# Multiplying the sub-keys into the query weights once, in a one-core mixer and product-key expert kernel

## The chip, the cores and the metric

The kernel runs on one core of a Trainium2 chip. The metric is the time of one execution on the device, in microseconds (us), as the median of the runs; lower is better.

## What is computed

One layer over 1,152 tokens (128 of a prompt, 1,024 of a sample), model width 1,024, all in float32. The part that matters here is the routing of the last block, which picks experts by product keys:

```python
def peer(h, w_pq, sub_keys, u_tab, v_tab):          # 8 heads, 2 halves of 128, 128 sub-keys, top 16
    q = (hf @ w_pq).reshape(T, PEER_HEADS, 2, PEER_HALF)
    s = jnp.einsum('thsd,hskd->thsk', q, sub_keys)   # scores: T x 8 x 2 x 128
    s_top, i_top = lax.top_k(s, PEER_TOPK)
    cand_s = s_top[:, :, 0, :, None] + s_top[:, :, 1, None, :]
    f_s, f_pos = lax.top_k(cand_s.reshape(T, PEER_HEADS, 256), PEER_TOPK)
    ...                                              # 128 experts for each token, softmax weights,
                                                     # gelu(u_tab[ids] @ x) weighted sum of v_tab[ids]
```

Before it stand the two mixers (a spatial-gating MLP and an attention with low-rank keys and values), the output product w_o, and a layer norm.

## The kernel before

The program has three parts, one behind the other, with a barrier between them. The work is written out by hand: each engine has its own order of steps, and semaphores join them.

**The mixers** (`mixer_inputs`). TensorE (PE) first makes the first third of the modulation from `w_mod` (four chunks of 2 MB, L545), then the keys and values of the cached context (`keys` L459, `values` L465), then for each of nine tiles of 128 tokens `project` (L481: z = h @ w_in, into banks 0 to 3) and `finish`. SyncE (SP) loads everything in the order of L236 to L252. From the point where the modulation is there, GpSimd (POOL) fills two large scratch tensors in DRAM with zeros (L279, 32 transfers of 768 KB, and L285, 16 of 512 KB), four of them in flight at a time. After the first tile ScalarE (ACT) stores two small outputs (L447, L448) and waits for them.

**The middle** (`middle`) is a loop over slots: slot n = 4i + h is head h of the attention of tile i. Beside the attention (`dots`, `turned`, `values`), each slot carries a piece of the later work of earlier tiles, in a fixed order on every engine: at h = 0 the product with w_o (`mix`, L846: 8 products of 512 columns for each half), at h = 2 the turning of the normed tile (`turn` L854, evicted by ACT's `modulate` L1038), and the routing in four groups g of four sub-key lists each:

- `query(i, g)`, L872: 32 products of 128 columns that give the queries turned, evicted by ACT into `qs` (L1052);
- `score(i, g)`, L882: 4 products of `qs` with the sub-keys `sub`, evicted by ACT into `s` (L1059);
- `lists(i, g)` on VectorE (DVE), L1265 and on: the top 16 of each list; and `decode(i)` at h = 0 of a later tile.

Groups 0 and 1 have their queries at h = 3, group 2 at h = 1, group 3 at h = 2. The score of groups 0 and 3 stands at h = 3, that of 1 at h = 0 of the next tile, that of 2 at h = 2. Banks 6 and 7 are used in turn by all of these steps, so each waits for the eviction of the step before the last. The weights of a step (2 MB: `w_mod2`, `w_o` or `w_pq`) are loaded by SP into one of two halves of `work`, when the step before the last has used it.

In `decode`, ACT's `spread` (L1070) copies list numbers for it; `norm` (L1105) scales an attention output that PE turns first thing in the next slot (L907). POOL places finished tiles' weights into the zeroed scratch with indirect DMAs (L161). At the end of this part PE's `scatter` (L943) and DVE's `one_hot` (L1371 to L1378) make two more tiles' blocks.

**The experts** (`experts`) stream the tables u and v through PE (L1624, L1638) and are not touched.

Of the kernel before, what the change touches and what calls it, by code (L numbers as in the profile page):

```python
# [15 lines left out]
F32 = mybir.dt.float32  # L16
# [7 lines left out]
P = 128  # L24
# [88 lines left out]
def build(nc, a):  # L113
# [11 lines left out]
    with es:  # L125
        x1_dram = nc.dram_tensor("x1_scratch", [T, D], F32, kind="Internal").ap()
        g_dram = [nc.dram_tensor("g_blocks", [CB, P, NKEY, TB], F32, kind="Internal").ap(),
                  nc.dram_tensor("g_cells", [GRID, 1], F32, kind="Internal").ap()]
# [39 lines left out]
def mixer_inputs(nc, a, sb, sem, PS, ident, modc, sp1, silu, slots, carry, work, big, krT, kT, vv, g_dram):  # L168

    with ExitStack() as c:  # L170
# [40 lines left out]
        hs = [hT[:, :, :], hT1]  # L211
        zero = free[:, D:D + ZW]
# [5 lines left out]
        ml = [sem(f"a_m{k}") for k in range(NM)]  # L218
        kl, zl = sem("a_kv"), [sem(f"a_in{n}") for n in range(len(Z))]
# [13 lines left out]
        with nc.Block() as block:  # L233
            @block.sync
            def _(sp):
# [195 lines left out]
            def _(act):  # L431
# [11 lines left out]
                act.activation(vv[:, 1, :], PS[6][:, :], ACT.Copy).then_inc(v_ev, 1)  # L443
                act_gelu(act, 0)
# [84 lines left out]
            def _(pe):  # L529
# [24 lines left out]
                values(pe, cckT)  # L554
                project(pe, 0, 0, first=True)
# [13 lines left out]
def middle(nc, a, sb, sem, PS, ident, modc, sp1, silu, slots, carry, work, first_in, big, krT, kT, vv, x1_dram, gate_dram, g_dram, placed):  # L569
# [7 lines left out]
    def number(*key):  # L577
        W[key] = len(W)
        if key[0] in ("mod", "mix", "query"):
            WEIGHTS.append(key)  # L580

    for n in range(NSLOT):
# [13 lines left out]
        if h == 0:  # L596
            if 0 <= i - 2 < NT:
                number("score", i - 2, 1)
            if 0 <= i - 1 < NT:
                number("mix", i - 1, 0)  # L600
                number("mix", i - 1, 1)
# [30 lines left out]
    with ExitStack() as c:  # L632
        wr = work[:, :].rearrange("p (b c) -> p b c", b=2)
        sub = sb(c, "sub", [P, HS, NKEY])
# [21 lines left out]
        qs = sb(c, "qs", [P, 2, 4, P])  # L656
# [63 lines left out]
        with nc.Block() as block:  # L720

            @block.sync
            def _(sp):
                def load(*key):
# [3 lines left out]
                    name = {"mod": "w_mod2", "mix": "w_o", "query": "w_pq"}[key[0]]  # L728
                    sp.dma_start(wr[:, at % 2, :], a[name][key[-1], :, :]).then_inc(wr_in[at % 2], 16)
# [7 lines left out]
                for n in range(NSLOT):  # L737
# [7 lines left out]
                    if n == 0:  # L745
                        for dst, src in ((ln_g, "ln1_g"), (ln_b, "ln1_b")):
                            sp.dma_start(dst[:, :], a[src]).then_inc(const_in, 16)
                        sp.dma_start(sub[:, :, :], a["sub"]).then_inc(const_in, 16)
# [5 lines left out]
                    if h == 1 and 0 <= i - 2 < NT:  # L754
                        load("query", i - 2, 2)
                    if h == 2 and 0 <= i - 2 < NT:
                        load("query", i - 2, 3)
                    if h == 3 and 0 <= i - 1 < NT:
                        load("query", i - 1, 0)
                        load("query", i - 1, 1)  # L760
# [10 lines left out]
                sp.wait_ge(w_mm, W["query", LAST, 3] + 1)  # L771
# [29 lines left out]
            def _(pe):  # L801
# [62 lines left out]
                def query(i, g):  # L864
# [3 lines left out]
                    w, ps = weights("query", i, g), bank("query", i, g)  # L868
                    for l in range(4):
                        for k in range(DK):  # L870
                            at = (l * DK + k) * P
                            mm = pe.matmul(ps[:, l * P:(l + 1) * P], w[:, at:at + P], slots[:, i, k * P:(k + 1) * P],  # L872
                                           start=(k == 0), stop=(k == DK - 1))
                    mm.then_inc(w_mm, 1)

                def score(i, g):
                    ps = bank("score", i, g)
                    pe.wait_ge(*emptied("query", i, g))
                    if i == 0 and g == 0:
                        pe.wait_ge(const_in, 48)  # L880
                    for l in range(4):
                        mm = pe.matmul(ps[:, l * NKEY:(l + 1) * NKEY], qs[:, g % 2, l, :], sub[:, 4 * g + l, :],  # L882
                                       start=True, stop=True)
# [64 lines left out]
                for n in range(NSLOT):  # L948
# [21 lines left out]
                    if h == 0:  # L970
                        if 0 <= i - 2 < NT:
                            score(i - 2, 1)
                        if 0 <= i - 1 < NT:
                            mix(i - 1, 0)
                            mix(i - 1, 1)
                    if h == 1 and 0 <= i - 2 < NT:
                        query(i - 2, 2)
                    if h == 2:
                        if 0 <= i - 2 < NT:
                            score(i - 2, 2)  # L980
# [3 lines left out]
                        if 0 <= i - 2 < NT:  # L984
                            query(i - 2, 3)
                    if h == 3:
                        if 0 <= i - 2 < NT:
                            score(i - 2, 3)
# [3 lines left out]
                        if 0 <= i - 1 < NT:  # L992
                            query(i - 1, 0)
                            query(i - 1, 1)
                            score(i - 1, 0)
                    if n == NH + 2:
# [9 lines left out]
            def _(act):  # L1006
# [38 lines left out]

                def query(i, g):
                    ps, f = bank("query", i, g)
                    n = 4 * i + g
                    if n >= 2:
                        p = ("score", (n - 2) // 4, (n - 2) % 4)  # L1050
# [1006 lines left out]
```

## Time and profile before

| what | value |
| --- | --- |
| median of 3 runs | 3407.02 us (3401.91 to 3409.48) |
| the profiled execution | 3406.51 us, its span 3404.4 us |
| PE busy over the span | 3273.6 us (96%) |
| DVE, POOL, ACT busy | 2590.0, 1564.4, 1238.5 us |
| the mixers | 0 to about 363 us |
| the middle | about 363 to 1233 us |
| the experts | about 1233 to 3404 us |
| L872 (queries), PE | 2304 instructions, busy 263.5 us |
| memory read, written | 888.70 MB, 61.24 MB |

The span is the time from the first to the last instruction; some 2 us of the execution lie around it. A float32 product is two instructions in the trace (32 products are x64). The end of a product is modelled, so the pace of PE is read from the start of one group to the start of the next.

### The profile page before, as it was taken

To read this page: it belongs to the slowest core of one execution; us is meant where nothing else is said; L and a number is where in the kernel's file an instruction comes from. 1 tells how busy PE (TensorE), PEld (TensorE's weight loads), DVE (VectorE), ACT (ScalarE), POOL (GpSimd) and SP (SyncE) were. 2 spreads that over 40 slices of the span, in tenths; PEclk is the share of its full clock that TensorE was granted. 3 is DMA by queue.
4 is the path that set the end of the run, shared out by engine and by line. 5 is a ranking of instruction groups with operands and counts; after the bars stand their busy time and mean duration, and the time that the engine had idled before them with its cause. 6 is when DMAs were issued, how large, how long until landed. Compare 5 with 4: busy or idle time off the path is not lost.

```text
span 3404.4 us, 46351 instructions
## 1 busy us (share of the span) xinstructions
PE 3273.6 (96%) x17054; PEld 2753.7 (81%) x17054; DVE 2590.0 (76%) x5319; ACT 1238.5 (36%) x2289; POOL 1564.4 (46%) x969
## 2 busy tenths in 40 slices
PE   8999899999998779999999999999999999999997
PEld 3566358777876769999898999998999999999996
DVE  0232126888887879999999898889899998888866
ACT  1232233333432653333333333333433333333333
POOL 1100000578876428888788888433233332222201
PEclk9999999999999989999999999999999999999998
DMA  9600535666666579999999999998898999999943
GB/s 395 250 21 8 211 149 192 180 178 194 165 183 184 176 278 352 343 347 358 336 348 344 356 361 357 381 356 345 353 374 342 368 371 350 358 350 350 349 160 121
DMA packets 290762, 952.91 MB, mean 280 GB/s; under 512 B 92905, under 2 KB 146281, under 8 KB 231793
## 3 DMA queue, kind: packets, MB, share of 16 engines
q1 hardware_dynamic: 154322, 513.36, 40.6%
q0 software_dynamic: 135936, 436.53, 37.2%
q8 instruction: 132, 2.16, 0.2%
q14 instruction: 84, 0.69, 0.1%
q10 hardware_dynamic: 288, 0.16, 0.0%
HBM read 888.70 MB, written 61.24 MB: 279 GB/s over the span
## 4 chain that ended last, share of the span: by engine, by line
PE 57%; DVE 4%; DMA 2%; issue 0%; ACT 0%; SPq 0%; DVEq 0%; ACTq 0%
PE bank L1624 29%; PE bank L1638 28%; DMA work<-in_u 2%; DVE ring L1751 1%; DVE uL L1937 1%; DVE acc L1768 0%; DVE vL L1932 0%; DVE ga L1964 0%; ACT uR L1711 0%; DVE slots L1873 0%; DMA work<-x_scratch 0%; DVE cL L1929 0%; DVE st L1897 0%; DVE slots L1894 0%; DVE slots L1912 0%
## 5 line engine op out<-in xcount | busy, mean ns | idle before, releaser
L1585 POOL DMA_INDIRECT ring<-in_uv,slots x384 | 583.3, 1519 | 799.4 <-DVE carry L1768 686.6
L161 POOL DMA_INDIRECT g_cells<-slots x384 | 703.0, 1831 | 379.2 <-DVE slots L1350 260.5
L1624 PE MATMUL bank<-hR,uR 128*128 128x384 f32 x2048 | 690.1, 337 | 19.2 <-DVE uL L1937 19.2
L1624 PE MATMUL bank<-hR,uL 128*128 128x384 f32 x2048 | 690.0, 337 | 0.0
L1624 PE MATMUL bank<-hL,uR 128*128 128x384 f32 x2048 | 688.2, 336 | 0.0
L1697 ACT ACTIVATE cR<-ga 128x384 fp32r<-128x384 f32 x256 | 134.6, 526 | 946.2 <-PE bank L1638 691.0
L1638 PE MATMUL bank<-vR,cR 128*128 128x512 f32 x1536 | 477.5, 392 | 0.7 <-DVE slots L1873 0.7
L1638 PE MATMUL bank<-vR,cL 128*128 128x512 f32 x1536 | 476.0, 391 | 0.0
L1638 PE MATMUL bank<-vL,cR 128*128 128x512 f32 x1536 | 475.7, 391 | 0.0
L1751 DVE CUSTOM_DVE_ANT_0 ring<-ring,slots 128x1024 f32<-128x1024 f32 x384 | 467.7, 1255 | 0.0
L1624 PEld LDWEIGHTS bank<-hR,uR 128*128 128x128 f32 x2048 | 386.6, 189 | 31.1 <-DVE uL L1937 21.3
L1624 PEld LDWEIGHTS bank<-hL,uR 128*128 128x128 f32 x2048 | 386.4, 189 | 9.6
L1624 PEld LDWEIGHTS bank<-hR,uL 128*128 128x128 f32 x2048 | 385.9, 188 | 0.0
L1638 PEld LDWEIGHTS bank<-vL,cR 128*128 128x128 f32 x1536 | 288.3, 188 | 64.4
L1932 DVE TENSOR_TENSOR vL<-work,vR 128x1024 fp32r<-128x1024 f32 x256 | 313.1, 1223 | 34.1 <-ACT vR L1703 33.5
L1638 PEld LDWEIGHTS bank<-vR,cL 128*128 128x128 f32 x1536 | 288.2, 188 | 62.8
L1768 DVE SCALAR_TENSOR_TENSOR carry<-ring,cs,carry 128x1024 f32<-128x1024 f32 x254 | 326.4, 1285 | 9.1
L1937 DVE TENSOR_TENSOR uL<-work,uR 128x1024 fp32r<-128x1024 f32 x256 | 312.0, 1219 | 24.8 <-ACT uR L1711 24.7
L1638 PEld LDWEIGHTS bank<-vR,cR 128*128 128x128 f32 x1536 | 284.7, 188 | 44.2 <-issue 1.0
L1711 ACT ACTIVATE uR<-work 128x1024 fp32r<-128x1024 f32 x256 | 267.6, 1046 | 22.8 <-DMA work<-in_u 20.4
L872 PE MATMUL bank<-slots,work 128*128 128x128 f32 x2304 | 263.5, 276 | 7.3 <-ACT slots L1038 6.2
L872 PEld LDWEIGHTS bank<-slots,work 128*128 128x128 f32 x2304 | 260.3, 193 | 10.2 <-issue 8.0
(290 smaller groups left out, 4107.0 us busy)
## 6 DMA issues: line engine op xcount, KB each, us to landing
work<-in_u SPq DMA_DIRECT2D x256, 512.0 KB, 6.5
work<-in_v SPq DMA_DIRECT2D x256, 512.0 KB, 7.1
work<-in_w_pq SPq DMA_DIRECT2D x36, 2048.0 KB
work<-in_w_o SPq DMA_DIRECT2D x18, 2048.0 KB
g_cells<-work POOLq DMA_DIRECT2D x32, 768.0 KB, 7.3
work<-g_blocks SPq DMA_DIRECT2D x32, 768.0 KB, 13.5
work<-g_cells SPq DMA_DIRECT2D x32, 768.0 KB, 9.1
work<-in_w_mod SPq DMA_DIRECT2D x8, 2048.0 KB
```

The source lines that it names most:

```text
L161: pool.indirect_dma_start(out=cells_of(g_dram, i), out_offset=bass.IndirectOffsetOnAxis(ap=slots[:, i, D + k:D + k + 1].bitcast(U32), axis=0),
L872: mm = pe.matmul(ps[:, l * P:(l + 1) * P], w[:, at:at + P], slots[:, i, k * P:(k + 1) * P], start=(k == 0), stop=(k == DK - 1))
L1585: pool.indirect_dma_start(out=ring[:, k % R, :], out_offset=None, in_=a["uv"], in_offset=bass.IndirectOffsetOnAxis(ap=ids[:, k // P, k % P ...
L1624: mm = pe.matmul(A[t][:, 0:CW], w[:, t, k, :], h[:, k, :], start=(k == 0 and w is uR and h is hR), stop=(k == DK - 1 and w is uL))
L1638: mm = pe.matmul(ACC[2 * tt + half][:, :], w[:, t, tt * P:(tt + 1) * P], v[:, t, half * 512:(half + 1) * 512], start=(m == 0 and w is cR a ...
L1697: act.activation(cR[:, x % 2, :], ga[:, x % 2, :], ACT.Copy).then_inc(c_r, 1)
L1711: act.activation(uR[:, x % 2, :, :], uw[:, x % 2, :, :], ACT.Copy).then_inc(u_r, 1)
L1751: dve.tensor_tensor_reduce(out=ring[:, k % R, 0:D], in0=ring[:, k % R, 0:D], in1=whole(STILES[k // P]), scale=1.0, scalar=0.0, op0=ALU.mul ...
L1768: dve.scalar_tensor_tensor(accS[t], ring[:, k % R, D:2 * D], one, accS[t], ALU.mult, ALU.add).then_inc(v_done, 1)
L1932: dve.tensor_tensor(vL[:, x % 2, :], vw[:, VBUF[x], :], vR[:, x % 2, :].bitcast(F32), ALU.subtract).then_inc(v_l, 1)
L1937: dve.tensor_tensor(uL[:, x % 2, :, :], uw[:, x % 2, :, :], uR[:, x % 2, :, :].bitcast(F32), ALU.subtract).then_inc(u_l, 1)
```

## The change

The sub-keys are multiplied into the query weights once. Since s = (h @ w_pq) @ sub, the product w_pq @ sub of each list is formed in the mixers, behind `values` of the cached context and ahead of the first `project`, and written to a new scratch tensor in DRAM of 8 MB (`keys_scratch`). It is made in eight pieces of 1 MB: PE forms four banks of 512 columns of each piece (4 products of 128 columns a bank), ACT evicts them, stores the piece, and issues the load of the piece after the next. In the middle `query` and `qs` go; `score(i, g)` is now 8 products of 512 columns over the 1,024 model columns with the stored product as the moving operand, 2 MB of it loaded where `w_pq` was. Scores stand where the queries of the same group stood; lists and decoding stay in their slots. The load of `sub` moves from the middle to the mixers, ahead of `w_in`.

```diff
+                  nc.dram_tensor("keys_scratch", [4, P, DK * 512], F32, kind="Internal").ap()]
...
+        NPIECE = 8
+        piece = [flat[:, 8192:10240], big[:, 6144:8192]]
+        folded = [flat[:, b * 2048:(b + 1) * 2048] for b in range(2)]
+        sub = big[:, 8192:10240].rearrange("p (l k) -> p l k", l=HS)
...
(SP, mixers, behind the loads of w_kn, cckT, w_v)
+                sp.wait_ge(m_used, 2)
+                for p in range(2):
+                    sp.dma_start(piece[p], a["w_pqT"][p, :, :].rearrange("p (l d) -> p l d", l=4)).then_inc(ml[p], 16)
+                sp.wait_ge(m_used, 3)
+                sp.dma_start(sub[:, :, :], a["sub"]).then_inc(ml[2], 16)
                 for n, (at, w) in enumerate(Z):
                     sp.dma_start(w_in[:, :, at:at + w], a["w_in"][:, :, at:at + w]).then_inc(zl[n], 16)
...
(ACT, mixers)
+                for b in range(4 * NPIECE):
+                    p, k = divmod(b, 4)
+                    act.wait_ge(m_used, NM + b + 1)
+                    if k == 0 and p >= 2:
+                        act.wait_ge(fold_out[p % 2], fold_first[p % 2] + p // 2 * 16)
+                    act.activation(folded[p % 2][:, k * 512:(k + 1) * 512], PS[b % 4][:, :],
+                                   ACT.Copy).then_inc(m_row, 1)
+                    if k == 3:
+                        act.wait_ge(m_row, NM + b + 1)
+                        g, half = divmod(p, 2)
+                        act.dma_start(g_dram[2][g, :, half * 2048:(half + 1) * 2048], folded[p % 2]).then_inc(
+                            fold_out[p % 2], 16)
+                        if p + 2 < NPIECE:
+                            act.dma_start(piece[p % 2], a["w_pqT"][p + 2, :, :].rearrange(
+                                "p (l d) -> p l d", l=4)).then_inc(ml[p % 2], 16)
+                for k in range(2):
+                    act.wait_ge(fold_out[k], fold_first[k] + NPIECE // 2 * 16)
                 act_gelu(act, 0)
...
(PE, mixers)
                 values(pe, cckT)
+                pe.wait_ge(ml[2], 32)
+                for p in range(NPIECE):
+                    pe.wait_ge(ml[p % 2], (p // 2 + 2) * 16)
+                    for k in range(4):
+                        b = 4 * p + k
+                        pe.wait_ge(m_row, max(NM, NM + b - 3))
+                        for l in range(4):
+                            mm = pe.matmul(PS[b % 4][:, l * NKEY:(l + 1) * NKEY], piece[p % 2][:, l, k * P:(k + 1) * P],
+                                           sub[:, 4 * (p // 2) + l, :], start=True, stop=True)
+                        mm.then_inc(m_used, 1)
+                pe.wait_ge(m_row, NM + 4 * NPIECE)
                 project(pe, 0, 0, first=True)
...
(the order of the middle's steps; PE, ACT and SP follow it)
-            if 0 <= i - 2 < NT:
-                number("score", i - 2, 1)
...
         if h == 1 and 0 <= i - 2 < NT:
-            number("query", i - 2, 2)
+            number("score", i - 2, 2)
         if h == 2:
-            if 0 <= i - 2 < NT:
-                number("score", i - 2, 2)
...
             if 0 <= i - 2 < NT:
-                number("query", i - 2, 3)
+                number("score", i - 2, 3)
         if h == 3:
-            if 0 <= i - 2 < NT:
-                number("score", i - 2, 3)
...
             if 0 <= i - 1 < NT:
-                number("query", i - 1, 0)
-                number("query", i - 1, 1)
                 number("score", i - 1, 0)
+                number("score", i - 1, 1)
...
(PE, middle)
-                def query(i, g):
+                def score(i, g):
                     if g == 0:
                         pe.wait_ge(*emptied("turn", i, 0))
                         pe.wait_ge(*emptied("turn", i, 1))
...
+                    w, ps = weights("score", i, g), bank("score", i, g)
+                    for k in range(DK):
+                        mm = pe.matmul(ps[:, :], slots[:, i, k * P:(k + 1) * P], w[:, k * 512:(k + 1) * 512],
+                                       start=(k == 0), stop=(k == DK - 1))
                     mm.then_inc(w_mm, 1)
...
(ACT, middle: query and its evictions into qs go; the score evictions move with the scores)
-                    act.activation(qs[:, g % 2, :, :], ps[:, :].rearrange("p (l t) -> p l t", l=4),
-                                   ACT.Copy).then_inc(f, 1)
...
-        "w_pq": n["w_pq"][0].reshape(DK, P, 4, 4, P).transpose(2, 1, 3, 0, 4).reshape(4, P, 4 * DK * P),
+        "w_pqT": n["w_pq"][0].reshape(2, 512, 4, 4, P).transpose(2, 0, 4, 3, 1).reshape(8, P, 4 * 512),
```

## Rows read from the trace of the kernel before

**Rows 1.** Busy time by window in the middle; the first line names the columns.

```profile
core 0: us, PE busy (x) PEld busy (x) DVE busy (x) ACT busy (x) POOL busy (x), PEclk, DMA share, GB/s
765.00:850.00 85.00, 83.92 (x526) 65.85 (x526) 69.87 (x311) 29.97 (x73) 71.29 (x46) 1.00 0.70 195
1020.00:1105.00 85.00, 68.51 (x482) 58.13 (x483) 67.64 (x320) 23.95 (x51) 58.69 (x38) 0.92 0.63 179
```

**Rows 2.** Waits of PE from 510 to 1020 us: total us, times, longest.

```profile
PE bank L872 <- ACT slots L1038: 5.0, 6, 0.8
PE bank L854 <- ACT carry L1059: 1.8, 7, 0.3
```

**Rows 3.** Timeline of PE over one tile: start us, us, instruction.

```profile
753.21 1.06 PE L882 MATMUL bank<-sub,qs 128*128 128x128 f32 x8
754.10 3.60 PE L846 MATMUL bank<-work,slots 128*128 128x512 f32 x8
...
760.97 3.60 PE L846 MATMUL bank<-work,slots 128*128 128x512 f32 x8
...
774.81 7.31 PE L872 MATMUL bank<-slots,work 128*128 128x128 f32 x64
781.96 0.27 PE L907 MATMUL bank<-ident,on 128*128 128x128 f32 x1
...
789.83 0.60 PE L854 MATMUL bank<-ident,xr 128*128 128x128 f32 x4
...
792.17 7.38 PE L872 MATMUL bank<-slots,work 128*128 128x128 f32 x64 [0.83 <-ACT slots L1038]
```

**Rows 4.** Timeline of ACT in the same tile.

```profile
780.30 0.37 ACT L1105 ACTIVATE on<-bank,ri 128x128 f32<-128x128 f32 x1
...
787.78 1.06 ACT L1070 ACTIVATE key<-itb 128x1024 bf16<-128x1024 bf16 x1 [0.16 <-DVE itb L1276]
```

**Rows 5.** Timeline of DVE in the same tile.

```profile
808.52 0.87 DVE L1265 MAX8 top<-carry 128x8 f32<-128x128 f32 x4 [3.36 <-ACT carry L1059]
```

**Rows 6.** Timeline of PE at the end of the middle.

```profile
1065.45 7.41 PE L872 MATMUL bank<-slots,work 128*128 128x128 f32 x64 [1.06 <-DMA work<-in_w_pq]
...
1136.14 3.81 PE L943 MATMUL bank<-big,krT 128*128 128x128 f32 x32 [2.23 <-ACT krT L1132]
```

**Rows 7.** Timeline of PE in the mixers.

```profile
43.43 3.65 PE L459 MATMUL bank<-cckT,work 128*128 128x128 f32 x16 [0.58 <-DVE sp L377]
...
48.64 23.36 PE L481 MATMUL bank<-w_in,carry 128*128 128x512 f32 x64
...
100.90 1.95 PE L459 MATMUL bank<-ckT,work 128*128 128x128 f32 x16
...
122.64 7.83 PE L481 MATMUL bank<-w_in,carry 128*128 128x384 f32 x14 [3.69 <-DVE work L333]
```

**Rows 8.** Windows of 4 us in the mixers (the last two columns: DMA share, GB/s).

```profile
60.00:64.00 4.00, 4.00 (x12) 1.91 (x11) 0.80 (x4) 0.60 (x1) 1.07 (x2) 1.00 1.01 422
136.00:140.00 4.00, 3.93 (x34) 3.74 (x33) 2.81 (x10) 0.00 (x0) 0.00 (x0) 1.00 0.34 134
```

**Rows 9.** DMA, 0 to 170 us: POOL's queue (packets, MB, share); issues (KB, us to landing).

```profile
q0 software_dynamic: 6912, 33.56, 48.8%
...
g_cells<-work POOLq DMA_DIRECT2D x32, 768.0 KB, 7.3
...
out_new_krope<-kr ACTq DMA_DIRECT2D x1, 32.0 KB, 11.1
```

**Rows 10.** DMA queues, 55 to 56 us: packets, MB, share of the engines' time.

```profile
q0 software_dynamic: 45, 0.26, 61.6%
q1 hardware_dynamic: 45, 0.17, 40.5%
```

**Rows 11.** DMA queues, 108 to 109 us.

```profile
q0 software_dynamic: 27, 0.14, 49.2%
q1 hardware_dynamic: 74, 0.20, 48.7%
```

More of the change, by code:

```diff
@@ L578, in number @@
         W[key] = len(W)
-        if key[0] in ("mod", "mix", "query"):
+        if key[0] in ("mod", "mix", "score"):
             WEIGHTS.append(key)
@@ L727, in load @@
                         sp.wait_ge(w_mm, W[WEIGHTS[at - 2]] + 1)
-                    name = {"mod": "w_mod2", "mix": "w_o", "query": "w_pq"}[key[0]]
-                    sp.dma_start(wr[:, at % 2, :], a[name][key[-1], :, :]).then_inc(wr_in[at % 2], 16)
+                    src = {"mod": a["w_mod2"], "mix": a["w_o"], "score": g_dram[2]}[key[0]]
+                    sp.dma_start(wr[:, at % 2, :], src[key[-1], :, :]).then_inc(wr_in[at % 2], 16)
                 def load_x(i):
@@ L754, in _ @@
                     if h == 1 and 0 <= i - 2 < NT:
-                        load("query", i - 2, 2)
+                        load("score", i - 2, 2)
                     if h == 2 and 0 <= i - 2 < NT:
-                        load("query", i - 2, 3)
+                        load("score", i - 2, 3)
                     if h == 3 and 0 <= i - 1 < NT:
-                        load("query", i - 1, 0)
-                        load("query", i - 1, 1)
+                        load("score", i - 1, 0)
+                        load("score", i - 1, 1)
                         sp.wait_ge(x1_ready, i)
@@ L770, in _ @@
                             sp.dma_start(gate_dram[m, :, :], gl[:, m, :]).then_inc(gate_out, 16)
-                sp.wait_ge(w_mm, W["query", LAST, 3] + 1)
+                sp.wait_ge(w_mm, W["score", LAST, 3] + 1)
                 for k in range(2):
@@ L969, in _ @@
                                 second(2 * n)
[L970 to L975, printed above, removed]
+                    if h == 0 and 0 <= i - 1 < NT:
+                        mix(i - 1, 0)
+                        mix(i - 1, 1)
                     if h == 1 and 0 <= i - 2 < NT:
-                        query(i - 2, 2)
+                        score(i - 2, 2)
                     if h == 2:
-                        if 0 <= i - 2 < NT:
-                            score(i - 2, 2)
                         if 0 <= i - 1 < NT:
@@ L984, in _ @@
                         if 0 <= i - 2 < NT:
-                            query(i - 2, 3)
+                            score(i - 2, 3)
                     if h == 3:
-                        if 0 <= i - 2 < NT:
-                            score(i - 2, 3)
                         if i - 2 in STILES:
@@ L992, in _ @@
                         if 0 <= i - 1 < NT:
-                            query(i - 1, 0)
-                            query(i - 1, 1)
                             score(i - 1, 0)
+                            score(i - 1, 1)
                     if n == NH + 2:
@@ L1148, in _ @@
                         root(i - 1)
-                    if h == 2:
-                        if 0 <= i - 2 < NT:
-                            score(i - 2, 2)
-                        if 0 <= i - 1 < NT:
-                            modulate(i - 1, 0)
-                            modulate(i - 1, 1)
+                    if h == 2 and 0 <= i - 1 < NT:
+                        modulate(i - 1, 0)
+                        modulate(i - 1, 1)
                     if n + 1 < NH:
@@ L1166, in _ @@
                             use(2 * n)
-                    if h == 0 and 0 <= i - 2 < NT:
-                        score(i - 2, 1)
                     if h == 1 and 0 <= i - 2 < NT:
-                        query(i - 2, 2)
+                        score(i - 2, 2)
                     if h == 2 and 0 <= i - 2 < NT:
-                        query(i - 2, 3)
+                        score(i - 2, 3)
                     if h == 3:
-                        if 0 <= i - 2 < NT:
-                            score(i - 2, 3)
                         if i - 2 in STILES:
@@ L1179, in _ @@
                         if 0 <= i - 1 < NT:
-                            query(i - 1, 0)
-                        if 0 <= i - 1 < NT:
-                            query(i - 1, 1)
                             score(i - 1, 0)
+                            score(i - 1, 1)
                     if n == NH + 2:
```

42 lines of the change are left out of this document (10 added, 32 removed).

## The prediction

> **What bounds the kernel now.** I first cut the span into windows. In the middle the busy time of PE is 83.92 of 85 us at full clock, that of DVE 69.87, of ACT 29.97; near its end, from 1020 us, PE has only 68.51 [rows 1]. A busy PE can hide waits, so I read its waits next: from 510 to 1020 us they come to 6.8 us in all, 1.3% [rows 2]. So the loop over slots is set by PE's pace until the last tile, and what PE no longer does there is gained, unless another engine's chain comes up from behind. In the mixers I looked at PE's timeline and at the DMAs: PE goes on without a gap at 48.64 us into the first `project` [rows 7], while the transfers, POOL's zeros above all, fill the DMA engines (422 GB/s, share 1.01) until about 137 us [rows 8]. The zeros cost nothing today, for PE needs no transfer then. The change puts eight loads and eight stores of 1 MB on PE's path just there. So it gives in one part and takes in another, and the question is which is larger.
>
> **What the middle gains.** A group of queries is 64 instructions, from 774.81 to 781.96: 7.15 us [rows 3]. The new score of a group has the form of a half of `mix`, 8 float32 products of 512 columns with a token tile as the stationary operand: 754.10 to 760.97, 6.87 us [rows 3]. That is 0.28 us less, 36 times (9 tiles, 4 groups): 10.1 us. The old score goes: 753.21 to 754.10, 0.89 us, 36 times: 32.0 us. Together 42.1 us. The columns that stream are the same in the old query and the new score, 4,096 a group; this is why an edit that halves the steps gives 15% of them and not half.
>
> ACT loses 36 evictions; PE waited for none of them inside the loop [rows 2], so that is worth nothing but for the two waits named below. DVE no longer waits for the score of group 3 (3.36 us in this tile [rows 5]); that gives DVE slack.
>
> Two things take back from the 42.1:
> - At h = 2 PE turns the tile at 789.83 and starts the next group at 792.17 [rows 3], when ACT has evicted the first half. ACT comes to it from `spread`, 787.78 to 788.84 [rows 4], which hangs on DVE's chain. PE will be there 1.17 us earlier than now against that chain (0.89 + 0.28 since h = 0) and loses the score as well, so ACT is late: first half out at about 790.4, where PE alone would be some 0.3 us earlier. 7 tiles: 2 us.
> - In the tail a stretch is DVE's (layer norm of the last tile, then its lists), so the 1.17 us of one query and score are lost; the last score stands behind the first `scatter` at 1136.14, from which DVE's pace counts, 0.9 lost; and loads get tight: the one for 1065.45 already comes 1.06 us late [rows 6], and group 2 of the last tile is now needed some 6.9 us after its buffer is free instead of 8.9, so 1 us. Waits for `qs` that go give 1.4 back. Net 1.7 us.
>
> So the middle gains 42.1 − 2 − 1.7 = 38 us. Bounds: 42 if nothing is lost, 22 in a rival below.
>
> **What the mixers pay.** Nothing of the fold runs beside other PE work. Piece 0 is there in time: SP issues it when the second chunk of `w_mod` is used. Its products begin where `project` does now, at 48.6. A piece is 32 instructions of 128 columns, half of a query group: 3.6 us at full clock. PE alone would take 8 × 3.6 = 29 us. But pieces 2 to 7 come through ACT's queue, each behind a store: up to the landing of piece 7 the order is six pairs of store and load, 12 transfers of 1.05 MB. The first can start when piece 0 is made (52.2) and evicted, about 53; a load begins to move some 2 us after its issue, so I count from 55. With the engines to themselves each would take 1.05 MB at 422 GB/s = 2.5 us; but POOL always has four zero transfers in flight. How two queues share is seen when `xT` is loaded beside the zeros: 40.5% against 61.6% of the engines' time in one microsecond [rows 10], 48.7% against 49.2% in another [rows 11]. Half of the bandwidth gives 5.0 us a transfer. In the first of these, both queues got 45 packets, so the larger packet gets more: rows of 8 KB beside zeros of 6 KB would have 57%, 4.4 us. I take 4.7, in the middle between them: 12 × 4.7 = 56 us, piece 7 at 111.4.
>
> By the Trainium skill (DMA: Bandwidth & Descriptors, section Queues, rings and completion order) an engine goes round the queues by packets. The trace's 45 to 45 agrees and its 27 to 74 does not; by that rule alone the sum would be 12 × 0.3 = 4 us lower.
>
> PE now stands still some microseconds for each piece, and after such a pause it runs at the lower of its two clocks: 16 instructions of L459 took 3.65 us at 43.43, where the granted clock had fallen, and 1.95 at 100.90 [rows 7]. So piece 7 takes about 7 us: the fold ends at 118.4 and adds 118.4 − 48.6 = 70 us. Bounds: 43 with the engines to itself (12 × 2.5, and 7), 89 in the rival of the long queue.
>
> The first `project` may start at the low clock: 0 to 4 us, I take 2. The last two stores need not be waited for by PE: ACT waits for them, and its first gelu is needed only by the second `project`, 23 us later [rows 7]. SP issues `w_in` (7 MB) only when the third chunk of `w_mod` is used; at 0.42 MB/us it needs 17 us and has 70; the fold hides it, and would not if it took under some 10 us. The zeros end later: 14.7 MB of ACT's queue (eight stores, six loads) at 0.42 MB/us is 35 us, and what is left of `w_in` some 7, so near 179 instead of 137, still long before POOL is needed in the middle. That has a good side. Today ACT's small store of the first tile falls among the zeros, lands after 11.1 us [rows 9], and PE waits 3.69 us for what is behind it and then runs slowly, 14 products in 7.83 us [rows 7]. With the change this store comes at about 175 to 180, when the zeros are over or nearly so: gain 0 to 7, I take 4.
>
> **The sum.** −38 + 70 + 2 − 4 = +30 us. The experts are untouched. The profiled execution took 3406.5 us (span 3404.4 and 2.1 around it), half a microsecond under the median of 3407.0; from the median it gives 3437 us, 0.9% slower. Its own range is 3425 to 3448 (4.4 to 5.0 us a transfer, and the ends of the small terms). A difference of 0.2%, 7 us, is what a measurement of this kernel can tell from none.
>
> **The rivals.**
> - *The fold's transfers are served first, not slower.* If ACT's queue gets nearly all the bandwidth, the fold adds 43 us: −38 + 43 + 2 − 4 = +3, 3410 us. It decides from a fold of 40 us on down. For it: ACT's packets are larger than the zeros', and up to four transfers of 1 MB are queued. Against it: both shares seen stay under one half. Chance 0.14.
> - *The long queue.* Each transfer waits behind what POOL has in flight. For it: 32 KB took 11.1 us to land, and a zero transfer of 768 KB 7.3 [rows 9]. Then a load behind its store lands after some 11 + 5 + 2 = 18 us, a round of two pieces takes 18 + 7 + 1 = 26, and the fold ends at 53 + 18 + 2 × 26 + 14 = 137: it adds 89, 3456 us. Against it: the queues shared in rows 10 and 11. Chance 0.15.
> - *DVE's chain takes over in the middle.* At the end of h = 1 `norm` is done at 780.67 [rows 4] and PE wants it at 781.96 [rows 3], 1.29 us later. With PE 1.17 us earlier the slack is 0.1. Tiles whose decoding is longer, or ACT a step later, would wait 2 us a tile: 16 us of the gain are lost, 3453 us. Chance 0.10.
> - *Wide products are much cheaper.* If PE's pace is set by the instruction and not by its columns, the 16 instructions of a group at 7.15 / 64 = 0.112 us take 1.8 us, and 36 × 5.1 = 182 us more are gained: 3255 us. Against it: the 16 of L846 take 6.87 us, 0.43 each, four times the columns at four times the time [rows 3]. Chance 0.01. The Trainium skill has a milder form of this (TensorE: Matmul & The Clock Gate, section Back-to-back issue gap: about 131 ns at 512 columns beside 81 ns at 128). By its pair a group would take an estimated 2.9 us and the kernel 3294 us; the row of L846 does not agree.
>
> **Chances.** The forecast has 0.60. Of the first rival 0.05 lies under −0.2% and 0.09 within; with the last one: faster 0.06, within 0.2% 0.10, slower 0.84. The range runs from the first rival to the second, 3410 to 3458, and leaves out the far sides of both.
>
> **What would show it.** Right: L872 and `qs` gone, the score at 6.87 us a group, slots at h = 0 shorter by 0.9 and at h = 3 by 2.3; PE's first L481 near 118 us, with PE waiting for piece loads in between and a low granted clock; ACT's queue with 0.5 to 0.6 of the DMA share. Wrong: `project` before 92 or after 135 us; PE waiting for L1105 or L1038 by over 1 us in each tile.

## The result: 1.2% slower, +38 us

| what | value |
| --- | --- |
| kernel before, median of 4 runs | 3404.53 us (3401.91 to 3409.48) |
| changed kernel, median of 4 runs | 3442.84 us (3440.15 to 3454.76) |
| ratio, estimated from all runs | 1.0118, 95% interval 1.009 to 1.0145 |
| changed kernel again, beside the last experiments, median of 4 runs | 3445.95 us, ratio 1.0121 (1.0105 to 1.0136) |

The forecast was 3437 us, +30, with a range of 3410 to 3458. The profiled execution of the changed kernel was its longest, 3454.76 us (span 3452.8), so the account below has a second profiled execution of the same kernel beside it (3446.86 us). One execution of an experiment below, zeros_late, took 14927.77 us; its median there is of the other four. Each stretch ends where PE starts the first instruction of the next part.

| landmark | before | after | after, second | change | change, second |
| --- | --- | --- | --- | --- | --- |
| first `project` starts | 48.6 | 129.9 | 129.4 | +81.3 | +80.8 |
| first product of the middle's attention | 363.5 | 437.9 | 437.4 | −6.9 | −6.9 |
| first `scatter` | 1136.1 | 1180.3 | 1180.3 | −30.3 | −29.7 |
| experts start | 1238.9 | 1281.7 | 1281.7 | −1.4 | −1.4 |
| span | 3404.4 | 3452.8 | 3444.9 | +5.6 | −2.3 |

The last two columns are what each stretch adds. The first four stretches sum to +42.8 in both profiles. Only the experts, which the change doesn't touch, differ (2171.1 and 2163.2 us), so the 7.9 us between the two profiled executions are theirs.

**The fold.** PE's timeline in the mixers, changed kernel (start us, us, instruction; in brackets the wait before it). L592 is the fold, L511 is `project`, L489 and L495 are the keys and values of the cached context [rows 7]:

```profile
44.88 2.50 PE L489 MATMUL bank<-cckT,work 128*128 128x128 f32 x16 [0.58 <-DVE sp L390]
47.17 3.13 PE L495 MATMUL bank<-work,cckT 128*128 128x512 f32 x4
50.14 3.73 PE L592 MATMUL bank<-big,slots 128*128 128x128 f32 x32
53.71 3.74 PE L592 MATMUL bank<-big 128*128 128x128 f32 x32
68.29 6.34 PE L592 MATMUL bank<-big,slots 128*128 128x128 f32 x32 [10.84 <-DMA slots<-in_w_pqT]
77.96 6.62 PE L592 MATMUL bank<-big 128*128 128x128 f32 x32 [3.32 <-DMA big<-in_w_pqT]
90.08 5.72 PE L592 MATMUL bank<-big,slots 128*128 128x128 f32 x32 [5.50 <-DMA slots<-in_w_pqT]
98.81 3.84 PE L592 MATMUL bank<-big 128*128 128x128 f32 x32 [3.01 <-DMA big<-in_w_pqT]
111.90 6.71 PE L592 MATMUL bank<-big,slots 128*128 128x128 f32 x32 [9.25 <-DMA slots<-in_w_pqT]
122.84 6.38 PE L592 MATMUL bank<-big 128*128 128x128 f32 x32 [4.24 <-DMA big<-in_w_pqT]
129.91 23.47 PE L511 MATMUL bank<-w_in,carry 128*128 128x512 f32 x64 [0.69 <-ACT slots L462]
```

Each piece from the third on waits for its load, six waits and 36.2 us in all. Most waits cost twice: five of the six pieces behind them take 5.7 to 6.7 us, where the first two took 3.73. In stretches of these five the granted clock is 0.50 to 0.67 of full speed; only the piece at 98.81, after a wait of 3.01 us, has the full clock and takes 3.84. The fold takes 79.8 us in all; beside the waits and 29.4 us of products at full clock (no_transfers below) some 14 us are left, nearly all of it the price of the low clock. The windows show the mean granted clock beside full DMA engines (mean clock, DMA share and GB/s are the last three columns):

```profile
54.00:80.00 26.00, 11.84 (x72) 11.46 (x72) 0.00 (x0) 5.07 (x9) 3.19 (x6) 0.68 1.02 422
80.00:106.00 26.00, 14.13 (x89) 13.56 (x87) 0.00 (x0) 7.16 (x12) 3.19 (x6) 0.80 1.02 421
106.00:129.00 23.00, 12.86 (x64) 12.68 (x64) 0.00 (x0) 4.18 (x7) 2.65 (x5) 0.63 1.02 422
```

The engines move 422 GB/s as before [rows 8]. What changed is whose bytes they are. The DMA queues of the changed kernel, first from 54 to 110 us, then in two single microseconds, 92 to 93 and 98 to 99 (columns: packets, MB, share of the engines' time; q0 POOL's zeros, q10 ACT's stores and loads of the fold, q1 SP's loads, what is left of `w_in` and then the smaller ones behind it):

```profile
q0 software_dynamic: 1978, 10.79, 46.1%
q10 hardware_dynamic: 1441, 10.54, 44.6%
q1 hardware_dynamic: 1988, 2.26, 11.1%
...
q10 hardware_dynamic: 31, 0.25, 59.9%
q0 software_dynamic: 28, 0.17, 39.6%
q1 hardware_dynamic: 30, 0.01, 4.8%
...
q0 software_dynamic: 72, 0.39, 94.1%
q1 hardware_dynamic: 70, 0.01, 6.9%
q10 hardware_dynamic: 4, 0.00, 0.2%
```

While all three queues have work, each sends about the same number of packets (31, 30, 28), and ACT's queue, with the largest ones, has 0.25 MB in that microsecond. But over the 56 us it sent 1441 packets, the others 1978 and 1988. While it has work it is not served fewer packets, but it is empty or nearly so at times: at 77 to 79, at 88, and at 98 to 100. By 121 us it has sent 12.57 MB, the 12 transfers up to the load of piece 7, and PE starts that piece at 122.84. ACT's timeline shows why there are gaps:

```profile
54.54 0.35 ACTq L467 DMA_DIRECT2D keys_scratch<-slots  x1
54.93 0.76 ACTq L470 DMA_DIRECT2D slots<-in_w_pqT  x1
...
75.30 0.33 ACTq L467 DMA_DIRECT2D keys_scratch<-slots  x1
75.66 0.47 ACTq L470 DMA_DIRECT2D slots<-in_w_pqT  x1
```

L467 is the store and L470 the load; both are issued when a piece is multiplied and evicted. The first store is issued at 54.54, and ACT's queue sends its first packet between 57 and 58. Later the pair behind piece 2 is issued at 75.3, the older load is through at 77, and the queue sends hardly anything until 79.

**The middle.** PE's timeline in one tile, for [rows 3]; L876 is `mix`, L884 `turn`, L900 the new `score`, L925 stood at L907:

```profile
812.79 3.60 PE L876 MATMUL bank<-work,slots 128*128 128x512 f32 x8
...
826.52 0.27 PE L925 MATMUL bank<-ident,on 128*128 128x128 f32 x1
...
833.50 7.03 PE L900 MATMUL bank<-work,slots 128*128 128x512 f32 x16
840.54 0.30 PE L925 MATMUL bank<-ident,on 128*128 128x128 f32 x1
...
847.54 1.04 PE L884 MATMUL bank<-ident,xr 128*128 128x128 f32 x8
850.22 7.11 PE L900 MATMUL bank<-work,slots 128*128 128x512 f32 x16 [1.64 <-ACT slots L1048]
857.16 0.27 PE L925 MATMUL bank<-ident,on 128*128 128x128 f32 x1
...
864.13 13.90 PE L900 MATMUL bank<-work,slots 128*128 128x512 f32 x32
877.87 0.27 PE L925 MATMUL bank<-ident,on 128*128 128x128 f32 x1
```

Two groups go from 864.13 to 877.87, 6.87 us each. From 580 to 1060 us PE's waits are these, for [rows 2] (total us, times, longest):

```profile
PE bank L900 <- ACT slots L1048: 9.3, 6, 1.7
PE bank L925 <- ACT on L1106: 0.8, 1, 0.8
```

The end of the middle, PE's timeline, for [rows 6]; L891 turns a finished tile back, L961 is `scatter`:

```profile
1127.89 1.94 PE L884 MATMUL bank<-ident,xr 128*128 128x128 f32 x8 [8.57 <-DVE xr L1246]
1136.02 10.05 PE L900 MATMUL bank<-work,slots 128*128 128x512 f32 x16 [6.19 <-ACT slots L1048]
...
1149.11 13.97 PE L900 MATMUL bank<-work,slots 128*128 128x512 f32 x32 [1.70 <-ACT slots L1054]
1164.05 14.00 PE L900 MATMUL bank<-work,slots 128*128 128x512 f32 x32 [0.97 <-DMA work<-keys_scratch]
1180.28 1.91 PE L961 MATMUL bank<-big,krT 128*128 128x128 f32 x15 [2.23 <-ACT krT L1133]
```

For the same stretch of the kernel before, PE's longest waits from 1020 to 1140 us (total, times, longest; L1052 evicts the queries, L1059 the scores):

```profile
PE bank L854 <- ACT carry L1059: 6.0, 1, 6.0
PE bank L882 <- ACT qs L1052: 5.2, 3, 4.1
PE bank L854 <- DVE xr L1254: 2.5, 1, 2.5
```

### The profile page after: what moved, and what is told of

It is laid out like the page before. It is cut to its first block, busy times and chain, and to the rows that moved or that the text cites. A ratio compares the mean times of both kernels' runs of the same rounds, so it can differ in the third digit from the quotient of the medians.

```text
span 3452.8 us, 42789 instructions
## 1 busy us (share of the span) xinstructions
PE 3275.1 (95%) x15294; PEld 2611.3 (76%) x15294; DVE 2590.1 (75%) x5319; ACT 1237.8 (36%) x2285; POOL 1569.3 (45%) x969
## 4 chain that ended last, share of the span: by engine, by line
PE 48%; DVE 9%; DMA 4%; issue 1%; ACT 1%; SPq 0%; DVEq 0%; ACTq 0%
PE bank L1616 24%; PE bank L1630 24%; DMA work<-in_u 3%; DVE ring L1743 2%; DVE acc L1760 2%; DVE uL L1929 1%; DVE vL L1924 1%; DVE ga L1956 1%; DVE cL L1921 0%; ACT uR L1703 0%; ACT vR L1695 0%; DVE slots L1865 0%; DMA work<-x_scratch 0%; DVE st L1889 0%; DVE slots L1886 0%
## 5 line engine op out<-in xcount | busy, mean ns | idle before, releaser
L1703 ACT ACTIVATE uR<-work 128x1024 fp32r<-128x1024 f32 x256 | 267.8, 1046 | 37.8 <-DMA work<-in_u 35.8
L900 PE MATMUL bank<-work,slots 128*128 128x512 f32 x576 | 257.1, 603 | 22.2 <-ACT slots L1048 16.8
L1695 ACT ACTIVATE vR<-work 128x1024 fp32r<-128x1024 f32 x256 | 267.6, 1045 | 0.0
```

What stands on the lines that cost most here:

```text
L900: mm = pe.matmul(ps[:, :], slots[:, i, k * P:(k + 1) * P], w[:, k * 512:(k + 1) * 512], start=(k == 0), stop=(k == DK - 1))
L1695: act.activation(vR[:, x % 2, :], vw[:, VBUF[x], :], ACT.Copy).then_inc(v_r, 1)
L1703: act.activation(uR[:, x % 2, :, :], uw[:, x % 2, :, :], ACT.Copy).then_inc(u_r, 1)
```

## The experiments

Theory A, of the forecast: the change is two independent parts, a gain on PE in the middle and a loss in the mixers; the loss is transfers on PE's path that share the DMA engines with the zeros. Its rivals are that the parts touch each other, and that the fold is held by something else: a delay of each round, or its buffers.

Eleven kernels ran, each beside the kernel before on the same chip (its median: 3403.78 us beside the first four, 3404.07 beside deep_zeros_late and the kernels with swap but no stores4, 3403.39 beside the other three). "Fold" is the time from PE's first fold product to its first `project`; "to the middle" and "to `scatter`" are the next two stretches of the table above, 314.9 and 772.6 us in the kernel before. scores_only and no_transfers leave a part of the computation out.

| kernel | median us | ratio (95%) | fold | first `project` | to the middle | to `scatter` |
| --- | --- | --- | --- | --- | --- | --- |
| fold_only | 3474.16 | 1.0203 (1.0186 to 1.0221) | 79.7 | 129.8 | 308.0 | 772.6 |
| scores_only | 3369.77 | 0.9895 (0.9878 to 0.9911) | none | 49.1 | 314.1 | 740.6 |
| zeros_late | 3422.31 | 1.0049 (1.0033 to 1.0065) | 56.1 | 105.6 | 312.4 | 741.6 |
| no_transfers | 3396.01 | 0.998 (0.9971 to 0.999) | 29.4 | 79.1 | 309.7 | 741.1 |
| deep_zeros_late | 3417.25 | 1.004 (1.0026 to 1.0054) | 48.7 | 98.5 | 313.9 | 740.4 |
| stores4_late | 3416.45 | 1.004 (1.0027 to 1.0054) | 45.2 | 95.1 | 314.1 | 738.1 |
| after_swap | 3434.47 | 1.0089 (1.0073 to 1.0106) | 78.8 | 127.5 | 307.9 | 733.3 |
| before_swap | 3402.72 | 0.9993 (0.9983 to 1.0003) | none | 49.2 | 314.3 | 769.0 |
| deep_late_swap | 3411.54 | 1.002 (1.0011 to 1.003) | 48.1 | 97.2 | 313.9 | 737.5 |
| stores4_late_swap | 3409.61 | 1.0018 (1.0009 to 1.0027) | 44.9 | 94.2 | 314.1 | 733.9 |
| after_again | 3445.95 | 1.0121 (1.0105 to 1.0136) | 79.5 | 129.4 | 308.0 | 742.9 |

### Each part alone: fold_only and scores_only

The first is the kernel before with the fold added and its result used by nothing:

```diff
 (kernel before; SP, PE and ACT get the fold's steps as in the change)
+                pe.wait_ge(ml[2], 32)
+                for p in range(NPIECE):
+                    pe.wait_ge(ml[p % 2], (p // 2 + 2) * 16)
...
                 project(pe, 0, 0, first=True)
```

> The kernel before with the multiplying-in added to its mixers and its result not used: queries and scores stay as they were. Theory A (the whole loss is the fold, which waits for transfers that share the DMA engines with the zeros): the first project begins near 130 us as in the changed kernel, against 48.6; the stretch behind it is some 7 us shorter; total near 3404.5 + 81 - 7 = 3479 us. Rival B (part of what the changed kernel lost lies in its middle, in loading the scores' weights from scratch memory): less than that, 3450 to 3465 us.

The second is the change without the fold:

```diff
-                (the fold's steps on SP, PE and ACT)
...
-                    src = {"mod": a["w_mod2"], "mix": a["w_o"], "score": g_dram[2]}[key[0]]
+                    src = {"mod": a["w_mod2"], "mix": a["w_o"], "score": a["w_pq"]}[key[0]]
```

> The changed kernel without the multiplying-in: no pieces, no sub-keys; the scores' products read the query weights themselves (as many bytes in the same form), so their values are not scores. Theory A: from the first group's product to the first scatter 30 us less than before, from project to the middle as before; total near 3404.5 - 31 = 3373 us. Rival B (the middle gains nothing, or as much as was counted, 38): 3404 or 3366 us.

Measured: +70.4 and −34.0 us, together +36.4, beside +38.3 and +42.6 for the change in its two measurements. The parts add to 2 to 6 us less than the change, whose own two measurements differ by 4. fold_only has its first `project` at 129.8 and scores_only its stretch to `scatter` at 740.6, where the changed kernel has 129.9 and 742.4. What the middle gained and what the fold cost can be read apart.

### The zeros behind the fold: zeros_late

```diff
+                pool.wait_ge(m_row, NM + 4 * NPIECE)
                 for b in range(NZ):
                     if b >= 4:
```

> The changed kernel, with POOL's zero transfers held back until the fold's last eviction. Theory A (shared DMA engines): twelve transfers of 1.05 MB at 2.5 to 3.5 us, with w_in beside the first: project begins at 90 to 97 instead of 130 us; the small store of the first tile falls among the zeros again (7 us back); total near 3443 - 36 + 7 = 3414 us. Rival C (the fold is set by its own chain of landing, products, eviction and issue, with two pieces in the air, whatever else the engines carry): project at 115 us or later, total above 3430 us.

Measured: the first `project` at 105.6, between what the two theories asked for (90 to 97, and 115 or later), and 20 us off the time. PE's timeline:

```profile
66.34 6.41 PE L593 MATMUL bank<-big,slots 128*128 128x128 f32 x32 [9.54 <-DMA slots<-in_w_pqT]
72.70 3.84 PE L593 MATMUL bank<-big 128*128 128x128 f32 x32
81.39 5.74 PE L593 MATMUL bank<-big,slots 128*128 128x128 f32 x32 [4.85 <-DMA slots<-in_w_pqT]
```

The pieces now come in pairs some 15 us apart. The zeros are gone from the fold, and it still waits 19.7 us for loads, while the DMA engines have gaps. So the zeros cost 24 of the fold's 80 us (79.8 − 56.1), and a large part of the rest is not shared bandwidth.

### No transfers: no_transfers

```diff
-                    if k == 0 and p >= 2:
-                        act.wait_ge(fold_out[p % 2], fold_first[p % 2] + p // 2 * 16)
...
-                        act.dma_start(g_dram[2][g, :, half * 2048:(half + 1) * 2048], folded[p % 2]).then_inc(
...
-                            act.dma_start(piece[p % 2], a["w_pqT"][p + 2, :, :].rearrange(
```

> The changed kernel, its fold made from pieces 0 and 1 again and again, with no store and no further load; the scores read the query weights instead (values not scores, same bytes). Theory A: PE makes 256 instructions without a pause, 29 us, project at 79 to 82 us, zeros over at 137; total near 3443 - 49 + 5 = 3399 us. Rival D (ACT's evictions hold the fold up even without transfers): project after 90 us.

The scores read the query weights here, so their values are not scores. PE's last piece:

```profile
74.63 3.74 PE L580 MATMUL bank<-big 128*128 128x128 f32 x32
```

Measured: fold 29.4 us, `project` at 79.1, 3396.0 us. PE's part of the fold is 8 pieces of 3.57 us at full clock, as forecast. The other 50 us of the 80 hang on the transfers: the waits for them and the low clock behind the waits. It is also the bound: with transfers that cost nothing the change would gain 8 us.

### More buffers: deep_zeros_late and stores4_late

Four buffers for the pieces in place of two, all four loads issued at the start by SP, and the zeros late; then four buffers for the folded pieces too.

```diff
-        piece = [x.rearrange("p (l d) -> p l d", l=4) for x in piece]
+        piece = [x.rearrange("p (l d) -> p l d", l=4) for x in piece] + [kT[:, :, 2 * P:6 * P], kT[:, :, 6 * P:10 * P]]
...
-                        if p + 2 < NPIECE:
+                        if p + 4 < NPIECE:
...
 (stores4_late)
-        folded = [flat[:, b * 2048:(b + 1) * 2048] for b in range(2)]
+        folded = [flat[:, b * 2048:(b + 1) * 2048] for b in range(4)]
```

> The changed kernel with the zeros held back and four pieces in the air instead of two: pieces 0 to 3 are loaded from the start, each later one when the piece four before it is evicted. Theory E (beside the zeros, the fold was held by having only two pieces in the air: of the 56 us it took with the zeros held back, 29 are PE's products and the rest the wait for landings): project begins at 80 to 88 us instead of 105.6, total near 3422 - 21 = 3401 us. Rival F (it is bandwidth even so: stores, loads and w_in together fill the engines): project at 98 us or later, total 3415 us or more.

> As deep_zeros_late (four piece buffers, zeros behind the fold), and four buffers for the folded pieces in place of two, so that an eviction waits for a store only from the fifth piece on. Nothing is left out. Theory I (the two store buffers were what held deep_zeros_late back: its evictions waited 4 to 7 us five times for a store): the first project starts at 86 to 92 instead of 98.5, and the time is 6 to 12 us under that of deep_zeros_late, 3405 to 3411. Theory J (its stretch was already filled by transfers: the share of the DMA queues was about 1 up to 88): the project starts at 95 or later and the time is within 3 us of deep_zeros_late.

deep_zeros_late has `project` at 98.5, at theory F's number. But its pieces wait in another place. ACT's and PE's waits in it, from 50 to 130 us:

```profile
ACT slots L465 <- DMA keys_scratch<-slots: 24.8, 5, 7.3
...
PE bank L595 <- ACT slots L465: 12.3, 5, 5.6
```

No piece waits for its load any more; PE waits for an eviction, and that for a store out of one of the two `folded` buffers. I took those for the limit (theory I). stores4_late, with four, takes the wait away and has `project` at 95.1, only 3.4 us earlier, with the time within 1 us: theory J. Its DMA windows say what the limit is by then:

```profile
54.00:70.00 16.00, 14.18 (x112) 13.99 (x111) 0.00 (x0) 7.85 (x15) 0.00 (x0) 0.89 1.04 407
70.00:80.00 10.00, 7.25 (x63) 6.87 (x62) 0.00 (x0) 4.51 (x8) 0.00 (x0) 1.00 1.03 409
80.00:88.00 8.00, 2.33 (x20) 2.13 (x19) 0.00 (x0) 1.79 (x3) 0.00 (x0) 0.93 1.04 401
```

The engines are full up to 88 us with no zeros among the transfers: ACT's queue has 67.5% of them and SP's, with `w_in`, 35.8%. Pieces 4 to 7 still wait for loads, 10.2 us in all, and the last runs at the low clock:

```profile
87.72 6.70 PE L596 MATMUL bank<-big 128*128 128x128 f32 x32 [5.67 <-DMA big<-in_w_pqT]
```

So with the zeros gone and four buffers on each side, the bytes of the fold and of `w_in` leave a fold of 45 us, 16 more than PE needs, and 45 is more than the 32 to 35 that the middle gives (the last column against 772.6).

### The order of two steps on ACT: after_swap, before_swap, deep_late_swap, stores4_late_swap

In the middle PE waits for `modulate` (L1048), which stands behind `spread` at h = 2. Here it stands ahead:

```diff
-                    if 0 <= n - 2 * H - 1 < LAST * H:
-                        spread(*divmod(n - 2 * H - 1, H))
...
                     if h == 2 and 0 <= i - 1 < NT:
                         modulate(i - 1, 0)
                         modulate(i - 1, 1)
+                    if h == 2 and 0 <= n - 2 * H - 1 < LAST * H:
+                        spread(*divmod(n - 2 * H - 1, H))
```

> The changed kernel, with ACT's evictions of the turned tile placed ahead of its spread at h = 2. Theory G (PE's wait for the first half of these evictions, 9.3 us over six tiles and 6.2 in the tail, is ACT's order: spread hangs on DVE's chain): both waits fall to below 1 us a tile, the stretch from the first attention to the first scatter is 10 to 15 us shorter, total near 3443 - 12 = 3431 us. Rival H (DVE's chain gives the pace by then, so the wait moves to norm's output or to the next score): the stretch is shorter by less than 4 us.

> The kernel before with the same swap (its score of group 2 and the turned tile's evictions ahead of spread). Theory G: its waits of 5.0 and 1.8 us over the tiles and 6.0 in the tail fall, total 6 to 12 us less, near 3395 us. Rival H: within 3 us of the kernel before.

> All three together on the changed kernel: zeros held back, four pieces, the swap. If the parts add: 3401 - 12 = 3389 us, under the kernel before by 0.4%. If the swap gives nothing: 3401 us, no difference from before.

> The same with the modulation ahead of the spread on ACT in the middle. Nothing is left out. If the two parts add as they did in deep_late_swap: 5 to 6 us under stores4_late. By theory I that is 3399 to 3405, level with the kernel before; by theory J 3408 to 3414.

In the changed kernel it gives 8.4 us against the first measurement and 11.5 against the second; some 2 us of that are a first `project` that starts earlier, which the swap doesn't touch. In the kernel before it gives 1.3, which its interval can't tell from nothing. The stretch to `scatter` is 9.0 us shorter with it in the changed kernel and 3.7 in the kernel before, so most of what it mends was made by the change. Theory G asked for 10 to 15 us and waits under 1 us a tile, theory H for less than 4: neither came. Most of the gain is not in the loop, where I had looked for it: there the six waits for L1048 only fell from 9.3 to 7.5 us. From the first score to the last tile's slot after_swap gains 2.4 us, from there to `scatter` 6.6. Of these, 5.4 are the wait of 6.19 us at 1136.02 above, which is down to 0.83:

```profile
1124.03 9.58 PE L900 MATMUL bank<-work,slots 128*128 128x512 f32 x16 [0.83 <-issue]
```

In deep_late_swap and stores4_late_swap the swap gives 5.7 and 6.8. deep_late_swap came out at 3411.5 us, above both numbers asked of it (3389 and 3401); stores4_late_swap is at theory J's. These two are the best with the whole computation, and are still 0.2% slower than the kernel before, both intervals above 1. No version with the whole computation beat the kernel before; before_swap can't be told from the kernel before.

### The changed kernel once more: after_again

> The changed kernel once more, unaltered, for a second profiled execution of it beside the one of 3452.8. If that one's 12 us over the median lay in the fold or the middle, the account of the change by stretches has to be redone; if they lay in the experts' stretch (2171.1 there), this one has the first project at 128 to 131, the middle stretch at 741 to 743 and the experts' stretch shorter, 2157 to 2165, and the time is 3438 to 3446.

It came out so in each stretch; the account of the result uses it.

## Why the prediction was right, and where its terms were off

The direction held, and so did the two mechanisms, a gain on PE in the middle and a larger loss to the fold's transfers. The size is +38.3 and +42.6 us where +30 was forecast. It owes something to luck: the fold and the middle missed by 11.3 and 6.4 us in one direction, and the stretch behind the fold by 4.9 in the other. By the prediction's steps:

- **Pace of the new score: right.** 6.87 us a group forecast and measured. The products of 512 columns are no cheaper by the column; the last rival is out. Slots at h = 0 are 20.7 us where 21.6 was, at h = 3 20.7 where 23.05 was: 0.9 and 2.35 less, forecast 0.9 and 2.3. DVE's wait for the score of group 3 is gone.
- **The loop: right, 1 us short.** From the first group to the last tile's slot, 28 queries at 0.28 and 27 scores at 0.89 are 31.9 us; measured 28.8, so 3.1 lost where I had said 2. PE's waits for L1048 went from 5.0 to 9.3 us, at the place named and twice as large; waits of 1.8 for L1059 fell away [rows 2]. At some 1.5 us a tile they are over the 1 us that the prediction had named as a sign of being wrong: here its 0.3 us a tile was too small.
- **The tail: too small a loss.** The remaining 10.2 us of the 42.1 should have lost 1.7 and lost 7.3. PE's waits from the last tile's slot to `scatter` rose from 18.8 to 24.1. The step at fault: I let the last tile's 1.17 us of one group be lost and counted 1.4 us back for waits for `qs` that go. But PE has 4.4 us less to do between the last tile's slot and its turning (three queries at 0.28 and four scores at 0.89), and the stretch takes 54.5 us where it took 52.9. The 5.2 us of waits for `qs` are gone, and the wait for the layer norm has grown from 2.5 to 8.57: PE arrives earlier and waits for the same DVE chain. Behind it PE waits 6.19 for `modulate`, where it had waited 6.0 for L1059; on ACT both stand behind `spread`, which waits for DVE. Then the group runs at the low clock, 10.05 us for 16. Sum of the middle: −31.6 where −38 was forecast.
- **DVE's chain takes over: no.** PE waited once for L1106, 0.8 us. The slack of 0.1 held.
- **Transfers of the fold: the term that was off most.** 12 transfers from 55 us at 4.7 us each were to bring piece 7 at 111.4; it came at 122.8, 11.4 later. At 5.65 us each it looks like a wrong share. The queues say otherwise. The first packet left three microseconds later than I had counted, between 57 and 58. The twelfth transfer was through at about 121, and PE started piece 7 1.8 us later, a delay that I had not counted. Between 58 and 121 ACT's queue was empty for some 5 us in three gaps. What is left, 121 − 58 − 5 = 58 us for 12, is 4.8 each, close to the forecast's 4.7. So of the 11.4 us about 5 are the gaps, 3 the late start, 1.8 the end of the last load, and the rest is pace. The step that failed most is "the order is six pairs of store and load", taken as a queue that always has work. With two piece buffers and two store buffers the next pair is issued only when a piece is through PE and ACT, and with PE at the low clock that comes later than the queue can wait. zeros_late shows it from the other side: without the zeros the queue has still more gaps.
- **The long queue: not its mechanism, but near its number.** The first `project` at 129.9 lies nearer to this rival's 137 than to the forecast's 118.4, and a round of two pieces took 21.8 us, between the forecast's 18.8 and the rival's 26. The loads landed after 14.4 and 19.1 us (medians), as the rival had it (18). But ACT's transfers did not wait behind what POOL had in flight: in the microseconds with work in both queues they sent as many packets. The first rival's 92 is far off; its fold of 43 us is near the 45 of stores4_late, which has no zeros beside it.
- **How queues share.** I took the middle between half by time and a share by packet size. The microsecond shown above has 31, 30 and 28 packets. The Trainium skill (DMA: Bandwidth & Descriptors, section Queues, rings and completion order) says that an engine takes its queues in turn, by packets, and this trace agrees where all three have work. At 0.25 MB in that microsecond a transfer of 1.05 MB would take 4.2 us; but from 112 to 113, with 22, 24 and 25 packets and larger ones on SP's queue, ACT's queue has 0.18 MB, which is 5.8 us. The pace of 4.8 is a mean over both. That a third queue would take its turn beside the two was not in my sum, and over 54 to 110 us ACT's queue has 44.6% of the engines, where I had asked for 50 to 60.
- **Piece 7 at the low clock, 7 us: right** (7.07 to `project`). **The first `project` slow, +2: no**, its 64 products took 23.3 us as before.
- **Behind the fold: −6.9, forecast −2.** PE's wait of 3.7 us and the slow products behind it [rows 7] are gone, 3 us more than I took, and the +2 did not come. That it hangs on the zeros fits zeros_late, where they fall on that stretch again and it is 312.4 instead of 308.0, and scores_only, 314.1.
- **`w_in` and the zeros hidden: right for both.** PE waited for neither. But `w_in` was a third queue beside the fold: it was issued from 34.9 us on instead of 6.4, and its last part landed 56.1 us after its issue. In stores4_late SP's queue, with `w_in`, had 35.8% of the engines. What the fold takes without it was not tried. The zeros ended near 178 us, forecast 179.

Summed: the fold +11.3 and the middle +6.4 above the forecast, the stretch behind −4.9: +12.8, so +42.8 for what the change touches. The medians say +38.3 and +42.6.

Open: whether the three gaps would close with deeper buffers while the zeros stay where they are; the two were only tried together. And the gaps' 5 us are counted from single microseconds of one profile. Why the waits of the loop hardly shrank with the swap is open too.

## What to carry to other kernels

A precomputation that saves PE time on every tile must itself find cover: here 34 us saved in the middle were paid with 80 us in a place where PE had been running without a gap and the DMA engines were full. Before costing a chain of load, compute and store by bandwidth, ask how many transfers are issued ahead, since each one that waits for the compute adds its delay, and a wait of PE can bring the low clock for the next piece, here in five of six. And where two waits in a row hang on one slow chain, removing the first gives nothing and only lengthens the second, as with the waits for `qs` and for the layer norm here.

## What the runs showed of the hardware that was not expected

- Three DMA queues on the same engines sent about the same number of packets in a microsecond (31, 30 and 28), whatever their size, so bytes go by packet size: 0.25, 0.01 and 0.17 MB.
- From the issue of ACT's first store of 1 MB (54.54 us) to the first packet of its queue (57 to 58 us) about 3 us passed, with other queues busy; and from the last bytes of the load of piece 7 (about 121) to PE's first product of it (122.84) 1.8 us.
- The untouched stretch of the experts took 2171.1 and 2163.2 us in two profiles of one kernel, and 2156.9 to 2171.1 over all of the profiles. On its chain are pieces of 9 to 21 us that are loads of u, 2 to 11 of them in a run, and their number does not go with the span. Their cause is open.
